# Inverse roots by logarithm and exponential on ScalarE in a two-layer hybrid decoder step

## The reference

```python
y = xf * lax.rsqrt(jnp.mean(xf * xf, axis=-1, keepdims=True) + eps)                  # RMSNorm
y = (xf - mu) * lax.rsqrt(var + eps)                                                 # LayerNorm, group norm
kk = kk / jnp.maximum(jnp.sqrt(jnp.sum(kk * kk, axis=-1, keepdims=True)), 1e-12)     # keys in RWKV-7
```

## Time and profile before

| | |
|---|---|
| median of 3 runs | 4073.3 us (4068.99 to 4077.49) |
| profiled execution | 4074.64 us, of it the span of the trace 4072.9 us |
| mean granted TensorE clock | 0.922 of full speed |
| TensorE matmul busy | 3537.0 us, 87% of the span |
| VectorE busy | 1379.2 us, 34% |
| ScalarE busy | 807.4 us, 20% |
| POOL busy | 523.6 us, 13% |

### The profile page before, as it was taken

How to read it: one execution, slowest core, us unless ns; L and a number is a source line. 1 busy time by engine, 2 the same in 40 slices (tenths; PEclk the granted TensorE clock), 3 DMA queues, 4 the chain that set the end, 5 groups by cost and what they waited for, 6 DMA issues and landing times. The chain is left out here.

```text
span 4072.9 us, 66731 instructions
## 1 busy us (share of the span) xinstructions
PE 3537.0 (87%) x29134; PEld 2934.8 (72%) x29134; DVE 1379.2 (34%) x1966; ACT 807.4 (20%) x1428; POOL 523.6 (13%) x354
## 2 busy tenths in 40 slices
PE   5997884979999999699974499997877799999996
PEld 3665452669999999366532399997534499999995
DVE  1199546141111111400039644332373221111113
ACT  1000332031111111100125332332020121211111
POOL 0000210012212221000014311110000012222220
PEclk8998996989999999799986699998678899999998
DMA  1122531011111110122215412110110111111111
GB/s 74 52 41 95 166 125 54 30 42 38 53 46 39 55 47 27 42 73 73 73 40 200 151 43 55 43 43 16 44 36 32 36 37 47 43 51 42 42 50 56
DMA packets 192507, 239.68 MB, mean 59 GB/s; under 512 B 122323, under 2 KB 141524, under 8 KB 191220
## 3 DMA queue, kind: packets, MB, share of 16 engines
q1 hardware_dynamic: 183668, 205.99, 17.0%
q0 software_dynamic: 5120, 16.78, 1.2%
q10 hardware_dynamic: 3456, 12.98, 0.8%
HBM read 189.51 MB, written 46.20 MB: 58 GB/s over the span
## 5 line engine op out<-in xcount | busy, mean ns | idle before, releaser
L2457 PE MATMUL f_out<-f_u_hi,f_weights_hi 128*128 128x352 f32 x2112 | 685.5, 325 | 58.1 <-DVE f_u_lo L2499 58.1
L2458 PE MATMUL f_out<-f_u_lo,f_weights_hi 128*128 128x352 f32 x2112 | 680.5, 322 | 0.0
L2459 PE MATMUL f_out<-f_u_hi,f_weights_lo 128*128 128x352 f32 x2112 | 679.7, 322 | 0.0
L2433 POOL TENSOR_TENSOR f_weights_lo<-f_weights,f_weights_hi 128x1024 fp32r<-128x1024 f32 (+2 forms) x168 | 323.5, 1926 | 1932.6 <-ACT f_weights_hi L2469 1932.6
L2457 PEld LDWEIGHTS f_out<-f_u_hi,f_weights_hi 128*128 128x128 f32 x2112 | 399.3, 189 | 60.3 <-issue 48.8
L2458 PEld LDWEIGHTS f_out<-f_u_lo,f_weights_hi 128*128 128x128 f32 x2112 | 399.8, 189 | 0.0
L2459 PEld LDWEIGHTS f_out<-f_u_hi,f_weights_lo 128*128 128x128 f32 x2112 | 398.7, 189 | 0.0
L1230 PE MATMUL mp_out<-mp_mixed,mp_weights 128*128 128x352 f32 x1152 | 344.6, 462 | 41.5 <-DVE mp_mixed L1203 40.5
L2522 DVE TENSOR_TENSOR f_product<-f_out,f_gate 128x352 f32<-128x352 f32 x132 | 69.3, 525 | 882.7 <-PE f_out L2459 882.7
L2457 PE MATMUL f_out<-f_inner_hi,f_weights_hi 128*128 128x352 f32 x1056 | 341.4, 323 | 4.0 <-DVE f_inner_lo L2530 4.0
L1230 PEld LDWEIGHTS mp_out<-mp_mixed,mp_weights 128*128 128x128 f32 x1152 | 220.2, 191 | 165.9 <-issue 45.7
(11 more groups left out here) (359 smaller groups left out, 4986.1 us busy)
## 6 DMA issues: line engine op xcount, KB each, us to landing
f_weights<-in_w_gu SPq DMA_DIRECT2D x88, 512.0 KB, 3.7
scratch_rkv<-mp_out_tile ACTq DMA_DIRECT2D x24, 528.0 KB, 5.3
pc_rkv<-scratch_rkv SPq DMA_DIRECT2D x24, 528.0 KB, 6.3
f_weights<-in_w_down SPq DMA_DIRECT2D x48, 256.0 KB, 2.6
mp_weights<-in_w_rkv SPq DMA_DIRECT2D x24, 512.0 KB, 4.5
f_weights<-in_w_down SPq DMA_DIRECT2D x32, 320.0 KB, 2.9
all_hT<-in_x SPq DMA_DIRECT2D x2, 4224.0 KB, 13.1
all_hT<-in_cache_k SPq DMA_DIRECT2D x32, 256.0 KB, 4.9
```

What stands on the lines that cost most here:

```text
L2433: pool.tensor_tensor(lo[:, s, :w], raw[:, s, :w], hi[:, s, :w].bitcast(F32), ALU.subtract).then_inc(lo_ready, 1)
L2457: pe.matmul(out, hi[:, s, w], x_hi, start=(k == 0), stop=False)
L2458: pe.matmul(out, hi[:, s, w], x_lo, start=False, stop=False)
L2459: last = pe.matmul(out, lo[:, s, w], x_hi, start=False, stop=(k == parts - 1))
```

## The change

The inverse root is written as the exponential of minus half the logarithm: both on ScalarE, the logarithm reads the sum from PSUM and takes 1/count as its scale and epsilon as its bias (a column of three constants that is added to the constants; the columns behind it move by three). VectorE's scaling and its reciprocal go, and so does the square root. In prepare_chunks VectorE's floor moves ahead of the root: it reads the sums from PSUM by chunks with 1e-24 in place of 1e-12, ScalarE takes the logarithm by chunks in place, then the exponential. In the three plain norms logarithm and exponential go by chunks, all logarithms first, and VectorE's products go by chunks too, 24 instead of 8. Semaphores are renamed or dropped accordingly. The core of the diff (the constants and the semaphore lists are left out):

```diff
@@ -141,6 +142,7 @@
 
         self.ones, self.ident, self.rot = view("ones"), view("ident"), view("rot")
         self.causal, self.comb, self.headones = view("causal"), view("comb"), view("headones")
+        self.norm_eps, self.ln_eps, self.gn_eps = (view("eps")[:, i:i + 1] for i in range(3))
         self.map1, self.map2 = view("map")[:, 0:1], view("map")[:, 1:2]
 
 
...
@@ -239,8 +239,13 @@
                     if k >= 2:
                         act.wait_ge(summed, k - 1)
                     act.activation(sq[:, k % 2], src[:, k], ACT.Square).then_inc(squared, 1)
-                act.wait_ge(inv_ready, 1)
-                act.activation(rstd[:], inv[:], ACT.Sqrt).then_inc(rstd_ready, 1)
+                for n in range(NCH):
+                    act.wait_ge(summed, KD)
+                    act.activation(rstd[:, chunk(n)], sums[n][:, :TC], ACT.Ln, scale=1.0 / D,
+                                   bias=K.norm_eps).then_inc(logged, 1)
+                for n in range(NCH):
+                    act.wait_ge(logged, n + 1)
+                    act.activation(rstd[:, chunk(n)], rstd[:, chunk(n)], ACT.Exp, scale=-0.5).then_inc(rstd_ready, 1)
 
             @block.tensor
             def _(pe):
@@ -253,16 +258,11 @@
 
             @block.vector
             def _(dve):
-                dve.wait_ge(summed, KD)
                 for n in range(NCH):
-                    dve.tensor_scalar(rstd[:, chunk(n)], sums[n][:, :TC], 1.0 / D, NORM_EPS,
-                                      ALU.mult, ALU.add).then_inc(mean_ready, 1)
-                dve.wait_ge(mean_ready, NCH)
-                dve.reciprocal(inv[:], rstd[:]).then_inc(inv_ready, 1)
-                dve.wait_ge(rstd_ready, 1)
-                for k in range(KD):
-                    dve.scalar_tensor_tensor(dst[:, k], src[:, k], gain[:, k:k + 1], rstd[:],
-                                             ALU.mult, ALU.mult)
+                    dve.wait_ge(rstd_ready, n + 1)
+                    for k in range(KD):
+                        dve.scalar_tensor_tensor(dst[:, k, chunk(n)], src[:, k, chunk(n)], gain[:, k:k + 1],
+                                                 rstd[:, chunk(n)], ALU.mult, ALU.mult)
 
 
 def add_projection(nc, tag, rhs, kc, source, hT):
...
@@ -1044,19 +1043,19 @@
                 for h in range(AH):
                     pe.wait_ge(squared, h + 1)
                     if h >= 2:
-                        pe.wait_ge(taken, h - 1)
+                        pe.wait_ge(taken, (h - 1) * NCH)
                     for n in range(NCH):
                         last = pe.matmul(banks[h % 2][n][:, :TC], K.ones, sq[:, h % 2, chunk(n)], start=True, stop=True)
                     last.then_inc(summed, 1)
 
                 pe.wait_ge(shifted, 2 * BT)
-                pe.wait_ge(taken, AH - 1)
+                pe.wait_ge(taken, (AH - 1) * NCH)
                 for n in range(NCH):
                     for c in range(BT):
                         last = pe.matmul(banks[0][n][:, :TC], K.ones, mixT[:, AH + c, chunk(n)],
                                          start=(c == 0), stop=(c == BT - 1))
                 last.then_inc(summed, 1)
-                pe.wait_ge(taken, AH)
+                pe.wait_ge(taken, AH * NCH)
                 for c in range(BT):
                     pe.wait_ge(squared, AH + c + 1)
                     for n in range(NCH):
...
@@ -1071,14 +1070,25 @@
                         act.wait_ge(summed, h - 1)
                     act.activation(sq[:, h % 2], mixT[:, h], ACT.Square).then_inc(squared, 1)
                 for h in range(AH):
-                    act.wait_ge(inv, h + 1)
-                    act.activation(stat[:, h % 2], stat[:, h % 2], ACT.Sqrt).then_inc(rooted, 1)
+                    act.wait_ge(summed, h + 1)
+                    if h >= 2:
+                        act.wait_ge(read, h - 1)
+                    for n in range(NCH):
+                        act.activation(stat[:, h % 2, chunk(n)], banks[h % 2][n][:, :TC], ACT.Ln, scale=1.0 / P,
+                                       bias=K.ln_eps).then_inc(taken, 1)
+                    act.wait_ge(taken, (h + 1) * NCH)
+                    act.activation(stat[:, h % 2], stat[:, h % 2], ACT.Exp, scale=-0.5).then_inc(rooted, 1)
                 for c in range(BT):
                     act.wait_ge(centred, c + 1)
                     act.wait_ge(summed, AH + 1 + (c - 1 if c >= 2 else 0))
                     act.activation(sq[:, c % 2], mixT[:, AH + c], ACT.Square).then_inc(squared, 1)
-                act.wait_ge(inv, AH + 1)
-                act.activation(stat[:, 0], stat[:, 0], ACT.Sqrt).then_inc(rooted, 1)
+                act.wait_ge(summed, AH + 1 + BT)
+                act.wait_ge(read, AH)
+                for n in range(NCH):
+                    act.activation(stat[:, 0, chunk(n)], banks[1][n][:, :TC], ACT.Ln, scale=1.0 / (BT * P),
+                                   bias=K.ln_eps).then_inc(taken, 1)
+                act.wait_ge(taken, (AH + 1) * NCH)
+                act.activation(stat[:, 0], stat[:, 0], ACT.Exp, scale=-0.5).then_inc(rooted, 1)
                 for c in range(BT):
                     act.wait_ge(read, AH + c + 1)
                     act.activation(mixT[:, AH + c], mixT[:, AH + c], ACT.Silu,
...
@@ -1092,15 +1102,6 @@
                     dve.tensor_scalar(mixT[:, AH + c, TP:], mixT[:, AH + c, TP:], cb[:, c:c + 1], None,
                                       ALU.add).then_inc(shifted, 1)
                 for h in range(AH):
-                    dve.wait_ge(summed, h + 1)
-                    if h >= 2:
-                        dve.wait_ge(read, h - 1)
-                    for n in range(NCH):
-                        last = dve.tensor_scalar(stat[:, h % 2, chunk(n)], banks[h % 2][n][:, :TC], 1.0 / P, SUBLN_EPS,
-                                                 ALU.mult, ALU.add)
-                    last.then_inc(taken, 1)
-                    dve.wait_ge(taken, h + 1)
-                    dve.reciprocal(stat[:, h % 2], stat[:, h % 2]).then_inc(inv, 1)
                     if h == 0:
                         dve.wait_ge(gain_ready, 1)
                     dve.wait_ge(rooted, h + 1)
...
@@ -1114,14 +1115,6 @@
                 dve.wait_ge(shifted, 2 * BT)
                 for c in range(BT):
                     dve.tensor_tensor(mixT[:, AH + c], mixT[:, AH + c], mean[:], ALU.subtract).then_inc(centred, 1)
-                dve.wait_ge(summed, AH + 1 + BT)
-                dve.wait_ge(read, AH)
-                for n in range(NCH):
-                    last = dve.tensor_scalar(stat[:, 0, chunk(n)], banks[1][n][:, :TC], 1.0 / (BT * P), LN_EPS,
-                                             ALU.mult, ALU.add)
-                last.then_inc(taken, 1)
-                dve.wait_ge(taken, AH + 1)
-                dve.reciprocal(stat[:, 0], stat[:, 0]).then_inc(inv, 1)
                 dve.wait_ge(rooted, AH + 1)
                 for c in range(BT):
                     dve.tensor_tensor(mixT[:, AH + c], mixT[:, AH + c], stat[:, 0], ALU.mult).then_inc(read, 1)
...
@@ -1382,11 +1375,11 @@
                     act.activation(sq[:], rkv[:, s, 1], ACT.Square, scale=col("kk")[:, ds(i, 1)]).then_inc(S["squared"], 1)
 
                 def tile(i):
-                    act.wait_ge(S["norm_sum"], i + 1)
-                    for n in range(NCH):
-                        act.activation(sq[:, chunk(n)], banks[n][:, :TC], ACT.Sqrt).then_inc(S["floor"], 1)
-                    act.wait_ge(S["floor"], START + i * NCH + NCH)
-                    act.sem_inc(S["rooted"], 1)
+                    for n in range(NCH):
+                        act.wait_ge(S["floor"], START + i * NCH + n + 1)
+                        act.activation(sq[:, chunk(n)], sq[:, chunk(n)], ACT.Ln).then_inc(S["logged"], 1)
+                    act.wait_ge(S["logged"], i * NCH + NCH)
+                    act.activation(sq[:], sq[:], ACT.Exp, scale=-0.5).then_inc(S["inv"], 1)
                     act.wait_ge(S["lora_a"], i + 1)
                     act.wait_ge(S["t"], START + i)
                     act.wait_ge(S["m1"], START + i)
...
@@ -1430,10 +1422,9 @@
                         dve.wait_ge(S["Ep"], START + i)
                         dve.wait_ge(S["sig"], i * NCH + NCH)
                         dve.tensor_tensor_scan(cs[:], keep[:], sg[:], 0.0, ALU.mult, ALU.add).then_inc(S["cum"], 1)
-                        dve.wait_ge(S["rooted"], i + 1)
-                        dve.tensor_scalar(sq[:], sq[:], 1e-12, None, ALU.max).then_inc(S["inv"], 1)
-                        dve.wait_ge(S["inv"], i * 2 + 1)
-                        dve.reciprocal(sq[:], sq[:]).then_inc(S["inv"], 1)
+                        dve.wait_ge(S["norm_sum"], i + 1)
+                        for n in range(NCH):
+                            dve.tensor_scalar(sq[:, chunk(n)], banks[n][:, :TC], 1e-24, None, ALU.max).then_inc(S["floor"], 1)
                         dve.wait_ge(S["a"], i * NCH + NCH)
```

(48 more changed lines are left out.)

11 lines of the change are left out of this document (5 added, 6 removed).

## The result

The kernel after took 4039.8 us (median of 4 runs, 4036.15 to 4044.25), the one before beside it 4072.64 (4068.99 to 4077.49): a ratio of 0.9917, 95% interval 0.9903 to 0.9932. That is 33 us, where 62 were forecast, and outside the range of 3970 to 4033. Profiled, the span was 4038.7 us at a mean granted clock of 0.924, against 4072.9 at 0.922.

A forecast was written before the change was run, and what follows sets the result against it. Between the feed-forward stages TensorE waits for a VectorE, ScalarE, VectorE chain whose longest link is the reciprocal. Gains of 11.8, 8.8, 20.1 and 27 us less a 5 us loss sum to 62.7: from 4073.3 to 4011 us, range 3970 to 4033.

The forecast's parts named there:

- finish_heads term: In finish_heads a tile falls from 17.0 to 13.6 us, a gain of 27 us over eight tiles.
- The cold loop: Rival: finish_heads runs at 1.2 GHz throughout, 21 us a tile, total 4070 us, no change; chance 0.06 with parts of it.
- the ends that I had worked out: For finish_heads: a gain of 38 us at full clock, 11 at a granted clock of 0.72 (15.6 us a tile).
- the sign of a wrong size: The granted clock in finish_heads staying at 0.72 or below would show the forecast wrong in size.
- The table loads: At each root, logarithm and exponential each bring a 1.28 us load, some 36 more than before; chance 0.55, 3996 to 4035.
- The shared case: Rival: one table load serves both logarithm and exponential at each root, gain 92 us, total 3981 us; chance 0.32.
- Dear switches: Rival: a table switch holds ScalarE longer than 1.28 us; at 4.5 us the kernel takes about 4084 us; chance 0.03.
- Norms, finish_mix, prepare_chunks: Three plain norms gain 11.8 us, two feed-forward norms 8.8, finish_mix 20.1; prepare_chunks loses 5.

The follow-up runs named there:

- e2: Kernel after with five extra unused 128x352 products in finish_heads between the variance sum and the gate product: 4002.73 us, ratio 0.983.
- e8: Kernel after with a shared logarithm-exponential table loaded, behind the first two squares in norms and finish_mix; finish_heads' root ahead of the next square: 3955.5 us.
- e11: Kernel after with finish_heads' root ahead of the next tile's square, both table loads kept, the root's two waits in unchanged order: 3995.07 us.
- e4: Kernel after with a shared logarithm-exponential table loaded at the head of each norm, finish_mix, the finish_heads loop and each prepare_chunks tile: 3989.06 us.
- e3: Kernel after with a shared logarithm-exponential table loaded once, ahead of the finish_heads loop only: 4009.23 us, ratio 0.9841.
- e7: Kernel after, run once more without an edit: 4035.72 us, ratio 0.9919.
- e5: Kernel before with four extra unused products in finish_heads after the variance sum: 4075.36 us, ratio 1.0008.
- e1: Kernel before with only finish_heads (and the constant columns it reads) taken from the kernel after: 4070.43 us, ratio 0.9995.
- e10: Kernel after with finish_heads' root ahead of the next tile's square, both table loads kept, the root's two waits swapped: 4034.93 us.

## Why the prediction was wrong

**The step that failed** is the last of the finish_heads term: "a clock of 0.86, half way to full, adds 1.4: 13.6". No row gave the 0.86; the granted clock was 0.68, and the tile 17.2. The sum that stood ahead of it was good: 12.2 us at full clock (its steps add up to 12.0), and e2 measured 12.4 at a granted 1.00. I had argued that the gap between mean and variance goes and the products come closer. It does go, but the gap ahead of the gate grew from 1.57 to 3.89 us (my own steps gave 5.3 less 2.04, 3.3), and the gate behind it fell to 1.2 GHz in every tile; behind a gap of 1.63 it kept 2.4 in seven of the eight gates of e8 and six of the eight of e11. With 0.68 in place of 0.86 the forecast's own sum gives 16.3, and the gap of 3.9 in place of 3.3 adds 0.6. The 3.6 us that a tile took over the 13.6 would be 29 over the eight; 25 are lacking, and most of the other 4 lie in the last tile, which took 14.1 (from gate to gate, 3044.55 to 3058.61).

**The cold loop**, the rival given 0.06, was therefore the right mechanism with too high a price: 21 us a tile counts every product at 1.2 GHz, but the variance sum (1.94) and the first gate pair (1.06) still ran at or near 2.4. Of the ends that I had worked out, 15.6 us at 0.72 was the nearer one, and the 17.2 lie beyond it; I had taken the middle. What I named as the sign of a wrong size, a granted clock at 0.72 or below, is what came.

**The table loads** were read rightly from the loads at the tanh, the sigmoid and the squares. The shared case was worked out as a rival at 3981 us; e4, which makes it, took 3989.06, finish_heads gaining 33 us where I had 32, finish_mix 32 where I had 29, prepare_chunks 2 where I had 4. That the 33 and the 32 agree is luck: e3, with the same finish_heads, gained 25. The Trainium skill ("ScalarE: Activation LUTs", section "Table sets: the hidden batching unit") has both functions in one set: e3 and e4 agree with it, where that set was loaded neither function brought another load. That loads are placed for the longest run of functions, the other rule of the Trainium skill that the prediction weighed ("ScalarE activation tables: per-element evaluation and per-set limits", section "Table sets in the compiler and the runtime"), the trace after does not bear out: 85 loads, one at each logarithm and one at each exponential behind it.

**Dear switches** fell: the loads lasted 1283 ns each, and the next operation started 10 to 20 ns behind it (3005.68 + 1.28, then 3006.97).

**Norms, finish_mix, prepare_chunks** were right: -12.0 against -11.8, -9.2 against -8.8, +5.1 against +5. prepare_chunks lost by the steps that I had named (t 9.5 us behind the scan where I had 9.4, L1442 done at 19.6 where I had 19.5). finish_mix gave 2.6 more: 1.3 because the load of L1088 ran before the variance sums were done, where I had put it behind them, and most of the rest because the mean's sums took 7.3 us instead of the 10.03 that I had carried over.

**Attention** took 7.1 us more in the profiled execution, 4.6 in e7. In e2 and e3, with the same code up to there, it took what it took before, so it is of single executions and no part of the change, and it cannot account for the 25.

## What to carry to other kernels

When a long link is taken out of a chain, ask what TensorE does in the gap that remains: a price at 2.4 GHz holds only if the products behind the gap run at it, and the granted clock of the old stage says nothing for the new one. Slow products that cost nothing while another engine is the bound (the gate in e5) can cost the whole gain once it isn't (e1). Shortening the gap by moving one operation out of it (e11, 45 us under the kernel after) or filling it with unused products (e2, 37 under it) gave more here than the 33 of the edit itself, and functions that alternate are cheapest in one table, loaded where the engine waits anyway (e8).

## What the runs showed of the hardware that was not expected

- The tile's time does not fall evenly with the gap: 17.2 us at a gap of 3.9, 16.4 to 17.7 at 3.0 (e10, all but one tile), 10.5 to 10.6 at 1.6 (e11, the first five). Between them, at 1.7 to 2.5 us (e3), tiles of both kinds stand side by side, and even at 1.6 some gates fell.
- Where two waits stand ahead of an operation that needs a table, the load ran after the one written last, and the operation after both; swapping the two lines was worth 40 us. Where a single wait stands ahead, as at L244 of the plain norms, the load ran before it was over (32.67, the sums ending at 35.1).
